# Row fetches dealt unevenly over the dense products of an expert layer

## What is computed

```python
u = u_tab[eidx]
act = jax.nn.gelu(jnp.einsum('chkd,cd->chk', u, xb).astype(jnp.float32), approximate=False)
w = (g * act).astype(xb.dtype)
return jnp.einsum('chk,chkd->cd', w, v_tab[eidx])
```

## Time and profile before

| | us |
|---|---|
| median of 3 runs | 2061.41 (2059.48 to 2063.76) |
| the profiled execution's own time | 2062.45 |
| its span | 2060.7 |
| TensorE busy | 2020.1 (98%) |
| VectorE busy | 1509.1 (73%) |
| ScalarE busy | 994.8 (48%) |
| GpSimd busy | 1048.8 (51%) |
| granted TensorE clock, share of full | 0.996 |

### The profile page before, as it was taken

How to read it: one execution, slowest core, us unless ns; L and a number is a source line. 1 busy time by engine, 2 the same in 40 slices (tenths; PEclk the granted TensorE clock), 3 DMA queues, 4 the chain that set the end, 5 groups by cost and what they waited for, 6 DMA issues and landing times.

```text
span 2060.7 us, 31764 instructions
## 1 busy us (share of the span) xinstructions
PE 2020.1 (98%) x11815; PEld 1805.1 (88%) x11815; DVE 1509.1 (73%) x2840; ACT 994.8 (48%) x1825; POOL 1048.8 (51%) x615
## 2 busy tenths in 40 slices
PE   9999999999999999999999999999999999999998
PEld 8746889998999999999999999999867787877777
DVE  6237548979898478889999999997687635067763
ACT  4337433367789743333333333334556652256643
POOL 3212456764455577776766677674334444411242
PEclk9999999999999999999999999999999999999999
DMA  5330225776678899999999999996312222210021
GB/s 204 80 100 12 82 83 167 249 248 228 223 252 300 307 355 370 367 371 375 351 362 364 371 385 386 360 390 225 116 68 92 82 90 104 92 42 32 21 82 62
DMA packets 150936, 435.33 MB, mean 211 GB/s; under 512 B 14464, under 2 KB 61184, under 8 KB 148992
## 3 DMA queue, kind: packets, MB, share of 16 engines
q1 hardware_dynamic: 109312, 282.29, 39.2%
q0 software_dynamic: 41472, 151.01, 19.5%
HBM read 391.28 MB, written 41.97 MB: 210 GB/s over the span
## 4 chain that ended last, share of the span: by engine, by line
PE 77%; DVE 13%; issue 4%; DMA 3%; ACT 2%; POOL 1%; SPq 0%; DVEq 0%; ACTq 0%
PE bank L515 15%; PE bank L516 15%; PE bank L517 15%; PE bank L921 4%; PE bank L922 4%; PE bank L923 4%; DVE wide L2390 4%; PE bank L902 3%; DMA wraw<-in_wstream 2%; PE bank L1142 2%; PE bank L690 1%; DVE WTL L1917 1%; DVE fetched L2370 1%; PE wide L1165 1%; PE wide L1153 1%
## 5 line engine op out<-in xcount | busy, mean ns | idle before, releaser
L2712 POOL TENSOR_TENSOR wl<-wraw,wh 128x1024 fp32r<-128x1024 f32 x272 | 674.4, 2483 | 721.9 <-ACT wh L1330 720.2
L1330 ACT CAST wh<-wraw 128x1024 fp32r<-128x1024 f32 x360 | 374.7, 1045 | 179.5 <-PE bank L517 126.2
L515 PE MATMUL bank<-WTH,wh 128*128 128x368 f32 x1024 | 338.8, 331 | 11.8 <-issue 11.1
L515 PE MATMUL bank<-XH,wh 128*128 128x368 f32 (+2 forms) x976 | 344.6, 353 | 1.8 <-ACT wh L1330 1.1
L516 PE MATMUL bank<-XL,wh 128*128 128x368 f32 (+2 forms) x976 | 340.9, 349 | 0.0
L517 PE MATMUL bank<-XH,wl 128*128 128x368 f32 (+2 forms) x976 | 339.5, 348 | 0.0
L517 PE MATMUL bank<-WTH,wl 128*128 128x368 f32 x1024 | 337.5, 330 | 0.0
L516 PE MATMUL bank<-WTL,wh 128*128 128x368 f32 x1024 | 337.4, 329 | 0.0
L515 PEld LDWEIGHTS bank<-WTH,wh 128*128 128x128 f32 x1024 | 193.0, 188 | 16.2 <-issue 15.0
L921 PE MATMUL bank<-XH,wh 128*128 128x368 f32 x576 | 196.4, 341 | 8.5 <-issue 3.6
L515 PEld LDWEIGHTS bank<-XH,wh 128*128 128x128 f32 x976 | 183.4, 188 | 24.2 <-issue 4.8
(11 more groups left out here) (552 smaller groups left out, 3857.3 us busy)
## 6 DMA issues: line engine op xcount, KB each, us to landing
wraw<-in_wstream SPq DMA_DIRECT2D x360, 512.0 KB, 5.4
g_scratch<-gs SPq DMA_DIRECT2D x12, 2048.0 KB, 7.9
gr<-g_scratch SPq DMA_DIRECT2D x15, 1536.0 KB, 14.1
a_scratch<-tmp SPq DMA_DIRECT2D x72, 184.0 KB, 2.7
tmp<-a_scratch SPq DMA_DIRECT2D x46, 184.0 KB, 7.9
sq<-a_scratch SPq DMA_DIRECT2D x26, 184.0 KB, 8.8
shifted<-hc_scratch SPq DMA_DIRECT2D x12, 270.0 KB, 4.8
fetched<-in_u_rows,diag POOLq DMA_INDIRECT x144, 7.7
```

What stands on the lines that cost most here:

```text
L515: pe.matmul(o, w1, x1, start=n == 0, stop=False)
L1330: act.copy(wh[n % NSPLIT][:, :], wraw[n % NRAW][:, :]).then_inc(*w_hi.tell(n))
L2712: return pool.tensor_tensor(lo, src, hi.bitcast(F32), ALU.subtract)
```

## The change

The cost of a product in `fetch_schedule` is raised from 7 to 9, or from 10 to 12, for V products of groups after the tenth and U products of groups after the eleventh. These are the products from number 136, V(11,0), on. The total stays 251 picks and the last one still belongs to product 171.

```diff
     for what, n, i in expert_steps():
         if what == "V" or ORDER[n] >= SPILLED:
             crowded = what == "V" and n + 1 < N_GROUPS and ORDER[n + 1] < SPILLED
-            cost.append(0 if (what, n) == ("U", 0) else 7 if crowded else 10)
+            late = n > (10 if what == "V" else 11)
+            cost.append(0 if (what, n) == ("U", 0) else (9 if late else 7) if crowded else 12 if late else 10)
             if (what, n, i) == ("V", N_GROUPS - 2, 3):
                 last = len(cost)
```

## The result

The changed kernel takes 2066.22 us (median of 20 runs, 2060.61 to 2071.74) where the kernel before takes 2061.99 (20 runs, 2057.61 to 2069.25): a ratio of 1.0026, interval 1.0016 to 1.0036. It is slower by some 4 to 5 us. That lies in the stated range, 4 us above the forecast and just over the 0.2% that was to count as slower.

A forecast was written before the change was run, and what follows sets the result against it. TensorE, busy 98%, bounds the kernel, so only its gaps can change. Late +5.5 and early -4.7 give +0.8 us on the profiled 2062.45, or 2063.3; against the median, 2062.2 us, range 2055.5 to 2069.0.

The forecast's parts named there:

- no change: Whole kernel: late loss and early gain cancel, 2062.2 us against a median of 2061.41; chance 0.46.
- the rival in which VectorE sets the pace from product 136 on: Late part: no extra pick work falls in blocked time, early part returns only 3; +8, 2069.4 us; chance 0.20.
- The early part, -4.7 us: Before product 133: nine or ten picks fewer shrink TensorE's gaps; -4.7 us, bounds -1 and -9.
- The step by place: Early gaps: V(7,2) closes its 1.2 us, V(2,2) and V(5,2) together -1.0, V(9,2) +0.5.
- The late part, +5.5 us: 1253 to 1405 us: ten more picks make VectorE set the pace; 6.5 + 3 - 2 - 2, bounds +1 and +11.
- the larger of the two counts: Late part: DMA's term overlaps VectorE's and doesn't add, so DMA leaves 5.5 as it is.
- the DMA term: Late part: 62.7 MB at 392 GB/s takes 160 us, +8; buffers filled ahead and shifted edges give back some 4.
- the +3 for waits: Late part: about half of VectorE's 6.4 us idle is waits that more work can't fill, +3.
- the -2 for lag: Late part: VectorE reaches product 133 less late, and lag after product 171 costs nothing, -2.
- The 2 for blocked time: Late part: extra picks partly fill time VectorE is blocked beside POOL; 0 to 6.4 us, taken as 2.
- The law of the gaps: Before V(n,2): gap is evict lateness + 7.6 - 8.0 us with two picks, + 6.2 - 8.0 with one.
- the signs of being wrong: Late part keeps its 152 us, `WTL`'s mean drops near 0.9, or ACT waits over 10 us for `wraw`.

The follow-up runs named there:

- the second profile: The changed kernel run again without an edit: 2068.32 us, ratio 1.0031 to the kernel before; the profiled execution took 2065.28 us.
- The mirror: Costs 5 and 8 instead of 9 and 12 for late products, moving ten picks to the first 136: 2069.72 us, ratio 1.0038 to the kernel before.

## Why the prediction was right, and where not

The range held the result, and the change counts as slower, to which the prediction gave 0.28; "no change", at 0.46, was named likelier. The forecast came out 4 us low because one of its two terms was too small. What happened is the rival in which VectorE sets the pace from product 136 on (0.20); its 2069.4 is 3 us too high.

*The early part, -4.7 us.* In the two profiles of the changed kernel it gave 3.2 and 7.8 us, against one profile of the kernel before: the size is right for the kernel as it stood. The step by place is right for V(7,2): its evict starts 0.2 us after V(6,7) ended instead of 1.5, one pass of 1.3 us less, and the gap is gone. V(9,2), with its second pick, went from 1.57 to 1.26 us of idle time in the first profile and to 2.48 in the second; the forecast was +0.5. The 1.50 us before V(2,2) are gone, but those before V(5,2), which was to gain as well, grew from 0.64 to 1.75 and 1.18. For the rest, work taken from VectorE was only in part the reason: with the gate blocks in four parts, the same nine picks fewer give 0.6 us. The parts alone bring the early part from 519.9 to 512.2. That most of the gain of the change was less queueing behind gate blocks fits this, but was not tested by itself.

*The late part, +5.5 us: this term was mis-sized.* It is 12.4 and 9.1 us in the two profiles and 8.6 with four parts: inside the bound of +11 but for the first, which has the 20 us tile. The mechanism was right: with the fetches halved, where VectorE's excess stands alone, it costs 8.3 us. Right too was "the larger of the two counts": 8.3 and 4.1 alone, 8.6 together, and 4.1 is the "+8, give back some 4" of the DMA term. The step that failed lies in two entries of VectorE's sum. One is the +3 for waits: "about half" of its idle time was to be waits that more work can't fill, but in the windows with four parts all of it stayed, 6.3 us without the change and 7.3 with it. The other is the -2 for lag that "costs nothing" at the end. The chain before V(14,2) comes ahead of product 171, and the lag came due there: 3.17 us of idle time, 1.3 more than before (2.4 more with four parts). The prediction's own signs had this gap growing; its sum did not. Redone over the windows with four parts, VectorE's 140.8 us and 10.3 for eight passes are 4.0 more than the 147.1 that the stretch took (the prediction had 6.5, with ten passes); with 7.3 of idle time, nothing given back for lag and 2.7 of blocked time the sum is 8.6, the 8.6 us by which the stretch grew. The 2 for blocked time was about right. The start of the last chain answers to the earlier trace rows:

```profile
1406.40 0.54 DVE L2442 TENSOR_TENSOR h<-bank,h 128x368 f32<-128x368 f32 x1
1406.85 2.67 DVE L2383 SCALAR_TENSOR_TENSOR wide<-fetched,diag,wide 128x1024 f32<-128x1024 f32 x2
```

From this evict to the restart at 1413.99 are 7.59 us, as in the two chains of two picks before (7.62 and 7.63), and 7.60 before V(12,2), which got its second pick by the change. The law of the gaps held: the evict starts 3.9 us after V(14,0) began on TensorE instead of 2.4, and 3.9 + 7.6 - 8.0 is 3.5, the 3.17 of idle time plus the start of the pipeline.

*The rule of the Trainium skill* (SBUF — State Buffer, "Who interferes with whom") was weighed rightly: extra picks did fill blocked time, as the gates show, but only 2.7 us of it where the prediction worked out up to 6.4 by that rule. On bandwidth the same skill (DMA: Bandwidth & Descriptors, "Bandwidth") gives about 358 GB/s when both cores of a pair stream and 435 as the ceiling of the ports. The 392 of the prediction and the 398 over 56 us here lie between the two, for a kernel on one core; so the 358 is not contradicted by them, it is the figure for another case.

*What would show it.* The gap before V(7,2) gone: yes. VectorE busy about 468 us in 704 to 1253: no, 477.62; from product 8 to 134 its busy time fell by 5.8 us (471.3 instead of 477.1), not by the 12 of nine passes. VectorE over 97% busy in the late window: no, 140.49 of 152 us, and 144.92 and 145.15 in the two other profiles, no more than before, since its idle time stayed and everything took longer. Gaps before V(11,2), V(12,2) and V(14,2) of 1.5 to 4 us: in the first profile 0.31, 2.57 and 3.17, in the second and with four parts all three. The early part 3 to 6 us ahead: yes, by 3.6 us at product 134, and 7.8 in the second profile. V(14,3) ending when it does now: no, TensorE restarts at V(14,2) 8.8 us later. Of the signs of being wrong none came: the late part didn't keep its time, `WTL`'s mean was 1.007 and 1.212 us, and ACT waited 8.9 and 4.4 us for `wraw` in the late windows, under the 10 that were to mean DMA.

## What to carry to other kernels

Where VectorE and the DMA queues are both within some 5% of TensorE's pace, as here, moving 4% of the work cost time in both directions: the gaps one sees in one part are not room in it. (The mirror was tried with whole gate blocks only, so that the even deal is the best one is not shown.) Don't count an engine's idle time as room before knowing what it waits for; here none of VectorE's was filled in the late part. When two limits are near, price each alone; here about the larger one counted, not their sum. Before dealing work anew, look for bursts: a 1.5 MB load cut in four and a pick put behind a gate gained 14 us where three changes of the schedule gained nothing. And take away the noise first: with the burst gone, the loss of the same change was 10 us with runs 5 us apart, instead of 5 us in runs 11 us apart.

## What was not expected of the hardware

A weight tile of 512 KB issued right behind a 1.5 MB block took up to 20.42 us to land where the median is 6.5. After some gaps (of 2.57 and 3.77 us in the changed kernel, of 1.88 at 894.82 in the one before) TensorE's granted clock was at its lower level for some ten of the next matmuls, 0.31 us apart instead of 0.166, which adds about 1.5 us; after the gap of 3.17 us at 1413.99 it was not, though it was after the one of 3.15 at the same place in the second profile, so the length of a gap alone doesn't tell. And the spread of a kernel's times fell with the queueing: 14.6 us between the fastest and slowest of 12 runs of the changed kernel, 4.7 over 12 with four parts; 11.6 over 20 runs of the kernel before, 4.1 over 6 with four parts.
